# Products on constants in seven places where TensorE waits, in a two-layer hybrid step with a mixture of experts

## The reference

```python
def _hier_moe(h, w_group, w_expert, w_gate, w_up, w_down):
    p_group = softmax(t @ w_group)             # 4 groups, the best one is taken
    e_logits = (t @ w_expert)                  # 8 experts in a group, the best two are taken
    w_top = softmax(top_v) * p_g
    hid = silu(t @ w_gate[e]) * (t @ w_up[e])  # 32 experts, 1024 -> 128
    out = sum over the two experts of w_top * (hid @ w_down[e])

for l in range(2):
    y = _ab_mixer(...) if l == 0 else _cd_mixer(...)
    x = layer_norm(ALPHA * x + gate * y)
    x = layer_norm(ALPHA * x + gate5 * _hier_moe(modulate(x)))
```

## Time and profile before

| | |
|---|---|
| median of three runs | 1292.52 us (1288.12 to 1296.45) |
| the profiled execution | 1289.75 us |
| its span, first to last instruction | 1287.9 us |
| mean granted clock of TensorE | 0.978 |
| PE busy | 1188.9 us (92% of the span) |
| DVE busy | 597.9 us (46%) |
| ACT busy | 352.0 us (27%) |
| DMA, mean over the span | 209 GB/s |

### The profile page before, as it was taken

One profiled execution on the slowest core, in us unless ns is written; L12 is line 12 of the kernel. 1 busy time (PEld: TensorE's weight loads), 2 busy tenths in 40 slices (PEclk: granted clock), 3 DMA queues, 4 the chain that ended last, 5 costly groups with the idle time before them and its releaser, 6 DMA issues.

```text
span 1287.9 us, 17510 instructions
## 1 busy us (share of the span) xinstructions
PE 1188.9 (92%) x6755; PEld 680.1 (53%) x6755; DVE 597.9 (46%) x1173; ACT 352.0 (27%) x695; POOL 186.9 (15%) x177
## 2 busy tenths in 40 slices
PE   5999999999999989999999877999999998999774
PEld 2554555545546577456555435755555555555441
DVE  2223333310136666768432217079986865332218
ACT  1333444421214543212122125311023111221122
POOL 1000000010000001131323120800000332222210
PEclk9999999999999999998999898999999998999988
DMA  9504476773211204826799969021114438999973
GB/s 348 210 25 177 142 254 239 289 270 114 89 33 40 74 10 163 340 83 232 299 407 409 406 244 393 23 91 66 66 66 171 156 128 316 392 410 408 354 293 150
DMA packets 99666, 269.79 MB, mean 209 GB/s; under 512 B 12811, under 2 KB 15154, under 8 KB 98690
## 3 DMA queue, kind: packets, MB, share of 16 engines
q1 hardware_dynamic: 83632, 234.55, 48.3%
q0 software_dynamic: 15632, 34.02, 7.1%
q10 hardware_dynamic: 322, 0.12, 0.0%
HBM read 257.68 MB, written 31.93 MB: 225 GB/s over the span
## 4 chain that ended last, share of the span: by engine, by line
PE 78%; DVE 6%; DMA 6%; SPq 4%; ACT 3%; issue 2%; ACTq 0%; POOLq 0%; DVEq 0%
PE ps L2285 18%; PE ps L2296 14%; PE ps L2797 8%; PE ps L2814 4%; PE ps L2175 4%; PE ps L2437 3%; DMA ln_rows<-in_moe_w_up 3%; PE ps L2600 3%; PE ps L2785 2%; PE ps L2581 2%; PE ps L2404 2%; PE ps L2746 2%; SPq L710 1%; PE ps L2699 1%; SPq L707 1%
## 5 line engine op out<-in xcount | busy, mean ns | idle before, releaser
L2285 PE MATMUL ps<-h_cm,weights 128*128 128x512 f32 (+1 forms) x832 | 226.8, 434 | 0.0
L2285 PEld LDWEIGHTS ps<-h_cm,weights 128*128 128x128 f32 x832 | 126.3, 191 | 104.0 <-issue 103.7
L2296 PE MATMUL ps<-weights,mix_cm 128*128 128x512 f32 x256 | 112.2, 595 | 0.0
L1769 DVE SCALAR_TENSOR_TENSOR scratch<-scratch,taps_cm 128x655 f32<-128x655 f32 x120 | 101.5, 897 | 2.5 <-ACT scratch L1325 1.0
L2296 PEld LDWEIGHTS ps<-weights,mix_cm 128*128 128x128 f32 x256 | 47.9, 190 | 56.5 <-issue 56.4
L2067 DVE TENSOR_TENSOR scratch<-ps,scratch 128x128 f32<-128x128 f32 x38 | 11.1, 292 | 143.1 <-ACT scratch L1373 143.1
L2296 PE MATMUL ps<-weights,h_cm 128*128 128x512 f32 (+1 forms) x208 | 71.4, 502 | 0.0
L2797 PE MATMUL ps<-weights,scratch 128*64 128x256 f32 x384 | 68.3, 389 | 1.8 <-DMA weights<-in_moe_w_up 1.8
L1442 DVE COPY mod_parts<-ps 128x512 f32<-128x512 f32 x24 | 16.6, 691 | 93.3 <-PE ps L2175 93.3
L1697 DVE SCALAR_TENSOR_TENSOR mix_cm<-mix_cm,gate_rows,ps 128x128 f32<-128x128 f32 x152 | 46.0, 345 | 25.1 <-PE ps L2545 23.0
L2296 PEld LDWEIGHTS ps<-weights,h_cm 128*128 128x128 f32 x208 | 36.3, 190 | 35.6 <-issue 35.6
(11 more groups left out here) (449 smaller groups left out, 2133.1 us busy)
## 6 DMA issues: line engine op xcount, KB each, us to landing
weights<-in_mod_w SPq DMA_DIRECT2D x13, 2048.0 KB, 8.9
x_tm<-in_mod_w SPq DMA_DIRECT2D x10, 2048.0 KB, 8.6
weights<-in_moe_w_gate SPq DMA_DIRECT2D x24, 512.0 KB, 11.6
weights<-in_moe_w_up SPq DMA_DIRECT2D x24, 512.0 KB, 13.4
weights<-in_moe_w_down SPq DMA_DIRECT2D x24, 512.0 KB, 15.7
scratch<-in_moe_w_down SPq DMA_DIRECT2D x21, 512.0 KB, 12.9
weights<-in_ab_w_in SPq DMA_DIRECT2D x5, 2048.0 KB, 12.8
weights<-in_cd_w_in SPq DMA_DIRECT2D x5, 2048.0 KB, 16.0
```

The costliest lines, as they stand in the source:

```text
L1769: ins = V.scalar_tensor_tensor(out=CO[:, j, 0:655], in0=UP[:, j, k:k + 655], scalar=CW[:, 4 * k + j:4 * k + j + 1], in1=CO[:, j, 0:655], o ...
L2285: ins = T.matmul(ps(*name)[:, a:b], w[:, k, col:col + 128], HT[:, k, a:b], start=(k == 0), stop=(k == KD - 1))
L2296: ins = T.matmul(ps(*name)[:, at:at + w.shape[2]], src[:, k, t * 128:t * 128 + 128], w[:, k, :], start=(k == 0), stop=(k == KD - 1))
```

## The change

A new helper, `keep_busy`, issues products of the identity on constants into a part of PSUM that the next real product overwrites; nobody reads them. It is called:

- ahead of the last logits of each layer, one product of 512 columns, before the wait for ACT's copy;
- ahead of pair 14 in layer 0 (five products of 256 columns) and of pair 13 in layer 1 (four), before the wait for the pair's weights, behind a wait on `hc` (the pair before the last has its hidden values copied);
- in layer 0's combination one product of 512 columns ahead of the turn of tile 0 and three ahead of that of tile 1, before the wait for the normed rows;
- in layer 1's combination four products of 512 columns ahead of the sum of tile 0, before the wait for the rows from HBM.

For all tiles of "ys", "xT" 1 and "lg" the opening of the group moves ahead of that wait.

```diff
+            def keep_busy(at, count):
+
+                for _ in range(count):
+                    T.matmul(at, ident, C[:, 0:at.shape[1]], start=True, stop=True)
+
             def mixed_sum(l, t):
 
+                open_group(pe, "ys", l, t)
+                if l and t == 0:
+                    keep_busy(ps("ys", l, t)[:, 0:512], 4)
                 pe.wait_ge(d_y[t], 32 * (l + 1))
-                open_group(pe, "ys", l, t)
...
             def x_turn1(t):
 
+                open_group(pe, "xT", 1, t)
+                keep_busy(ps("xT", 1, t)[:, 0:512], (1, 3, 0, 0, 0)[t])
                 pe.wait_ge(ln_normed, NT + t + 1)
-                open_group(pe, "xT", 1, t)
...
                 def router_product(t):
+                    open_group(pe, "lg", l, t)
+                    if t == 4:
+                        keep_busy(ps("lg", l, t)[:, 0:512], 1)
                     emptied(pe, "hT", l, t)
-                    open_group(pe, "lg", l, t)
...
                 main_turn(0)
                 for u in range(NP0):
+                    if (l, u) in ((0, 14), (1, 13)):
+                        pe.wait_ge(m["hc"], u - 1)
+                        keep_busy(pair_bank(u)[:, 0:256], 5 - l)
                     pe.wait_ge(pair_gu[u % PAIRS_IN_RING], 64 * uses(u, l))
                     gate_up(0, u, 2 * u)
```

## The result

The changed kernel takes 1297.73 us (median of 12 runs, 1294.87 to 1299.83), the kernel before 1292.68 us in the same series (12 runs, 1288.12 to 1296.45). The ratio is 1.0037 with a 95% interval of 1.0025 to 1.005: slower by 3.2 to 6.5 us, under 1%. The time lies just above the range given, and on the other side of the forecast.

What follows compares the result with a forecast made beforehand. PE was taken as the bound (busy 92%, 78% of the chain). Logits of layer 1 -0.6 and last combination -0.2 gave -0.8 us; about halfway to 2.9 is 2, so 1292.5 - 2 = 1290.5 us; range 1284 to 1297 us.

Steps and rivals of the forecast that it cites:

- The last logits: One product per layer in PE's wait for ACT: layer 0 gains nothing, layer 1 0.6 us; ends 0 and +0.6.
- The last sum: Layer 1's combination, four products ahead of the first sum: 4 of 8 records slow, -0.2 us taken.
- Rival (d): Four products ahead of the last sum end later than 1253.4: 1.6 or 3.3 us later, 1294 to 1296 us; chance 0.16.
- the upper end: Products ahead of layer 1's last sum: all eight records slow, 6.84 us, sum at full clock, 1.6 us later than before.
- Pairs: Pair 14 of layer 0: hidden, gain 0 (ends 0 and 2.3 us); pair 13 of layer 1: 1.7 us pushed in, cost 0.
- Turns of layer 0's combination: One product ahead of the first turn, three ahead of the second, hidden in waits: gain 0, at most 2.8 us.
- The 12.9 us: Whole kernel: most that the clock ramp would lose, from the skill's under 1% of a typical span.

Runs made afterwards that it cites:

- sum_only: Kernel before plus, of the change, only the four products ahead of the first sum of layer 1's combination: ratio 1.0031, +3.5 us.
- logits_only: Kernel before plus, of the change, only the product ahead of each layer's last logits: ratio 1.0032, median 1295.54 against 1291.55 us.
- count_fill_only: Kernel before with only seven instead of three products on constants ahead of the count products: ratio 1.0028, median 4.0 us over before.
- filled_three: Changed kernel with seven, not three, products ahead of the counts, none ahead of the last sum, three, not five, behind layer 0's broadcasts: ratio to before 0.9993.
- routing_only: Kernel before plus only the product ahead of the last logits and seven instead of three ahead of the count products: ratio 0.9989, 1.0 us under before.

## Why the prediction was wrong

- **The last logits: the step that failed.** "These 0.6 us go and DVE is next in line; they are passed on to the first experts." The first half came true: from the logits to the counts layer 1 took 9.10 us before (1063.70 to 1072.80) and 8.53 after (1067.13 to 1075.66). The second half left out PE itself. I asked what DVE reads earlier, and not what PE does with its time once the logits and the three products behind them are fast: it waits, 3.76 us instead of 0.40 and 1.03, and the clock falls directly ahead of 22 records that stand on the chain (layer 0) or among the first of them (layer 1). It cost 2.76 and 1.12 us in the profile, and +4.0 us when this part was alone. The low clock at the logits before had been the cheap place for it: DVE was busy there anyway, but for 0.62 us in layer 1, and the slow products filled the wait.
- **The last sum: the right mechanism, mis-sized.** That the broadcasts leave the clock low was right. The term "I take -0.2" should have been +3.3. By its working the sum would start 1.6 us later; it started 5.0 us later, for two reasons. I let the clock come back after 3.4 us of the products, from the stretch at 1217.3, so that four of eight records would be slow. In the profiles the eight records take 6.4 us (1254.98 to 1261.38 in the changed kernel; 1250.57 to 1256.81, 6.2 us, in sum_only), which is 1.3 us more. And I began them at 1248.0, where the broadcasts had ended before; in all three profiles with the four products the clock fell among the broadcasts (7.71, 7.87 and 8.17 us instead of 5.52), which is 2.2 us more in the changed kernel. These late broadcasts are not the change's doing: logits_only, count_fill_only, filled_three and routing_only have them, too (6.84 to 8.52 us), but there the wait for the rows swallows them, and the sum still starts about 5 us behind the first load. No profile shows four products behind broadcasts of 5.52 us, so what they cost then stays open. Rival (d), "3.3 us", has the right size and the right decision, the end of the products past the point of 1253.4 (1256.6 on the scale of before). Its sum is right by luck in part: it needed the sum's own records to be slow, and they were fast; the broadcasts were slow in their place. The nearest row was a stretch with products on 128 rows before and in it; for products behind one-row ones there was no row, and I should have kept the upper end as the likelier.
- **Pairs.** Right in both layers: the 1.7 us ahead of pair 13 came out of pair 14's wait (which shrank by 2.31 us, not by 1.7, as its weights were early), and from the first pair to the last turn nothing was lost but 0.26 us. In layer 0 a wait of 1.73 us was left behind 2.32 us of products, and no gain came of it. There, too, the low clock only moved, to pair 15.
- **Turns of layer 0's combination.** Right: with the clock high the projection waits for ACT (1.79, 1.06 and 1.01 us at 797.05, 802.79 and 808.49 in the changed kernel) and nothing is gained.
- **Range.** It ended at 1297 and the time is 1297.73. It had room for (d) alone; the routing had been bounded by +0.6 us.

The Trainium skill (TensorE: Matmul & The Clock Gate, section "What's actually happening"): that the number of slow matmuls differs from run to run agrees with the runs here. The mean granted clock of the kernel before lies between 0.970 and 0.981 in the 35 runs of one series. One profile of each kernel is kept, and the five products behind the broadcasts of layer 0 are slow in some of them and not in others, with no edit near them: the first sum came 14.0 us behind the last pair's turn in five of the eleven profiles that have these five, and 12.0 to 12.4 us in the other six. But the larger part isn't chance: the wait for the counts was 3.75 or 3.76 us and DVE's pass on the last sum 13.74 us in every profile with the edit in question. The 12.9 us that the prediction worked out from that section as a bound are not borne out: in the kernel before PE was busy at the low clock for about 37 us (30.4 us in the stretches from 602.9, 725.8, 790.6, 1063.8, 1217.3 and 1248.0 on, 6 to 7 us around 35 and 468), so by this estimate its work took about 18 us longer than at the full clock. How much of that is on the chain was not worked out.

## What to carry to other kernels

A product that only holds the clock moves the engine's idle time; it doesn't remove it. Follow it to the next wait on the same engine, and look there at the longer wait and at what the chain needs right behind it; then fill the whole stretch or leave it alone, since here each half alone cost 4 us and both together nothing. Ahead of data that the chain waits for, size such products by the low clock, not by the full one.

## What had not been expected of the hardware

One-row products (the broadcasts) neither held the clock nor brought it back here, while products on 128 rows brought it back. It fell in the middle of an unbroken series of them (0.82 in 1248 to 1252 of the changed kernel, 0.50 after it), and with four products on 128 rows strewn among them it stayed at the low level for 17 us of a PE that was never idle, rising only in the sum's products on 128 rows. It doesn't fall among them each time: in seven of the twelve profiles the eight records of layer 0 ran at the full clock throughout (3.7 us).
